# The last six output chunks of an MLP and their LayerNorm over three parts of the tokens in place of two halves, on one Trainium2 core

## The reference

```python
h = _layer_norm(ALPHA * h + (mix @ w_out + b_out), ln1_g, ln1_b)
f = jnp.square(jax.nn.relu(h @ w_mlp1 + b_mlp1)) @ w_mlp2 + b_mlp2
h = _layer_norm(ALPHA * h + f, ln2_g, ln2_b)          # y, 576 tokens x 1024

def _layer_norm(x, g, b):
    mu = jnp.mean(xf, axis=-1, keepdims=True)
    var = jnp.mean(jnp.square(xf - mu), axis=-1, keepdims=True)
    return (xf - mu) * lax.rsqrt(var + LN_EPS) * g + b
```

## Time and profile before

| | us |
|---|---|
| median of 3 runs | 827.62 |
| lowest, highest | 827.31, 828.57 |
| the profiled execution, device time | 829.96 |
| its span in the trace | 828.2 |
| its mean granted TensorE clock, share of full speed | 0.988 |

### The profile page before, as it was taken

How to read it: one execution, slowest core, us unless ns; L and a number is a source line. 1 busy time by engine, 2 the same in 40 slices (tenths; PEclk the granted TensorE clock), 3 DMA queues, 4 the chain that set the end, 5 groups by cost and what they waited for, 6 DMA issues and landing times.

```text
span 828.2 us, 14458 instructions
## 1 busy us (share of the span) xinstructions
PE 798.3 (96%) x5859; PEld 766.6 (93%) x5859; DVE 504.2 (61%) x844; ACT 390.8 (47%) x653; POOL 113.8 (14%) x134
## 2 busy tenths in 40 slices
PE   4899999999999999999999999999999999999994
PEld 2789879998988899999999999999999999999994
DVE  6753434546454456885868678774767877445454
ACT  4542425655555465563546664333554433344333
POOL 5230000190000000006550000000000000000452
PEclk9799999999999999999999999999999999999997
DMA  9503222112111202234111214222221422222202
GB/s 352 200 28 135 77 96 75 56 39 80 53 51 51 75 28 77 78 103 151 51 53 52 70 57 153 77 103 77 77 70 57 154 77 102 77 77 84 70 29 86
DMA packets 23082, 71.62 MB, mean 86 GB/s; under 512 B 2464, under 2 KB 6704, under 8 KB 22640
## 3 DMA queue, kind: packets, MB, share of 16 engines
q1 hardware_dynamic: 22192, 67.97, 24.5%
q0 software_dynamic: 544, 2.52, 0.9%
q10 hardware_dynamic: 288, 0.33, 0.1%
HBM read 65.96 MB, written 4.85 MB: 85 GB/s over the span
## 4 chain that ended last, share of the span: by engine, by line
PE 93%; DVE 5%; ACT 1%; DMA 0%; issue 0%; POOL 0%; ACTq 0%; DVEq 0%
PE lin L582 14%; PE lin L583 14%; PE lin L584 14%; PE z L1018 5%; PE z L1021 5%; PE z L1020 5%; PE lin L923 3%; PE lin L924 3%; PE lin L925 3%; PE z L797 3%; PE lin L1064 2%; PE lin L1063 2%; PE lin L1062 2%; PE z L783 1%; PE z L855 1%; PE z L584 1%
## 5 line engine op out<-in xcount | busy, mean ns | idle before, releaser
L582 PE MATMUL lin<-h_hi,whi 128*128 128x288 f32 (+1 forms) x832 | 247.2, 297 | 0.0
L583 PE MATMUL lin<-h_lo,whi 128*128 128x288 f32 (+1 forms) x832 | 245.9, 296 | 0.0
L584 PE MATMUL lin<-h_hi,wlo 128*128 128x288 f32 (+1 forms) x832 | 245.0, 294 | 0.0
L584 PEld LDWEIGHTS lin<-h_hi,wlo 128*128 128x128 f32 x832 | 156.6, 188 | 0.0
L582 PEld LDWEIGHTS lin<-h_hi,whi 128*128 128x128 f32 x832 | 156.5, 188 | 0.1
L583 PEld LDWEIGHTS lin<-h_lo,whi 128*128 128x128 f32 x832 | 156.4, 188 | 0.1
L1706 DVE TENSOR_TENSOR wlo<-raw,whi 128x1024 fp32r<-128x1024 f32 x65 | 80.9, 1245 | 34.9 <-ACT whi L1095 29.8
L1095 ACT ACTIVATE whi<-raw 128x1024 fp32r<-128x1024 f32 x58 | 60.9, 1051 | 51.1 <-PE lin L584 32.8
L1512 ACT ACTIVATE relu_t<-lin,vecs 128x288 f32<-128x288 f32 x60 | 30.0, 500 | 91.5 <-PE lin L584 88.1
L2133 DVE TENSOR_TENSOR relu_sq<-relu_t 128x288 f32<-128x288 f32 x60 | 27.5, 458 | 64.7 <-ACT relu_t L1512 64.7
L1018 PE MATMUL z<-f_ops,whi 128*128 128x288 f32 x216 | 64.2, 297 | 0.7 <-issue 0.7
(11 more groups left out here) (332 smaller groups left out, 1908.9 us busy)
## 6 DMA issues: line engine op xcount, KB each, us to landing
raw<-w_stream SPq DMA_DIRECT2D x88, 512.0 KB, 3.5
w_set<-w_sets SPq DMA_DIRECT2D x32, 384.0 KB, 3.6
r<-x_t SPq DMA_DIRECT2D x8, 296.0 KB, 5.6
y<-r SPq DMA_DIRECT2D x16, 144.0 KB, 1.9
kcache<-k_cache SPq DMA_DIRECT2D x1, 2048.0 KB, 13.9
vcache<-v_cache SPq DMA_DIRECT2D x1, 2048.0 KB, 10.5
k_new<-k_t POOLq DMA_DIRECT2D x1, 1184.0 KB, 4.8
v_new<-v_t POOLq DMA_DIRECT2D x1, 1024.0 KB, 5.7
```

Source lines behind the costliest of these rows:

```text
L582: pe.matmul(out, w_h, hi, start=first, stop=False)
L583: pe.matmul(out, w_h, lo, start=False, stop=False)
L584: return pe.matmul(out, w_l, hi, start=False, stop=last)
```

## The change

- Chunks 2 to 7 are worked on in three parts of the columns, 256, 176 and 144 wide (`PARTS2`), in place of two halves. Chunks 0 and 1 stay in halves. The products are `last_products`, the adds `add_part`, both counted by a semaphore `end_done`.
- Each part has its own sums and its own norm, interleaved on VectorE and ScalarE with the next part's adds and squares. The sums of parts 0 and 1 stand behind the first unit of the next part (`sums2`).
- In the last part GpSimd adds only up to chunk 5. Its sums, and chunk 6 with its squares, are taken up by TensorE between the products of the last unit (`last_sums`); only chunk 7 and its squares stand behind it (`last_term`, `last_square`).
- The last part's results stand in the same banks as part 0's, from column 320 on (`LATE2`). The variance is kept in PSUM (`r2_sq`) in place of SBUF (`var2`).
- The squares and sums of chunks 0 and 1 are made over the full width, once (`square2_first`, and the first two adds of GpSimd), in place of each half.
- There are 24 output DMAs in place of 16.

```diff
@@ -400,8 +402,17 @@
             return k % 6
 
         KEPT2 = 2
-        BY_DVE2 = (4, 6)
-        ADDS2 = (7, 6)
+
+        PARTS2 = (slice(0, 256), slice(256, 432), slice(432, TA))
+        LAST2 = len(PARTS2) - 1
+        BY_DVE2 = (4, 4, 6)
+
+        SUMMED2 = (KC, KC, KC - 2)
+
+        LATE2 = 320
+
+        def width2(p):
+            return PARTS2[p].stop - PARTS2[p].start
 
         def f_op(o, i, part):
 
...
+        def stat_cols(p):
+            at = LATE2 if p == LAST2 else 0
+            return slice(at, at + width2(p))
+
+        def r2_mean(p):
+            return z[:, p % 2, stat_cols(p)]
+
+        def r2_sq(p):
+            return xo[:, p % 2, stat_cols(p)]
+
+        def r2_rstd(p):
+            return small[:, stat_cols(p)] if p == 1 else z[:, 2, stat_cols(p)]
...
-            for h in range(2):
+            for p, c in enumerate(PARTS2):
                 for k in range(KC):
-                    sp.wait_ge(n2_out, KC * h + k + 1)
-                    sp.dma_start(y_out[:, k, half(h)], r2[:, k, half(h)]).then_inc(y_stored, 16)
-            sp.wait_ge(y_stored, 2 * 16 * KC)
+                    sp.wait_ge(n2_out, KC * p + k + 1)
+                    sp.dma_start(y_out[:, k, c], r2[:, k, c]).then_inc(y_stored, 16)
+            sp.wait_ge(y_stored, len(PARTS2) * 16 * KC)
...
+                    if ready is not None:
+                        pe.wait_ge(f_lo_done, ready(k))
+                    moving = f_hi[:, k, c], f_lo[:, k, c]
                     w_h, w_l = home[0][:, bass.ts(k, P)], home[1][:, bass.ts(k, P)]
-                    out = lin[:, bank, 0:HA]
                     pe.matmul(out, w_h, moving[0], start=k == 0, stop=False)
                     pe.matmul(out, w_h, moving[1], start=False, stop=False)
...
+                    last = pe.matmul(out, w_l, moving[0], start=False, stop=closes and k == KC - 1)
+                    if between is not None:
+                        between(k)
+                if not closes:
+                    pe.wait_ge(n2_first, 2)
+                    last = pe.matmul(out, ones_2[:, :], first_r2[:, c], start=False, stop=True)
+                return last
+
+            def sums2(p):
+
+                c = PARTS2[p]
+                pe.wait_ge(n2_sum[p], KC - KEPT2)
+                pe.matmul(r2_mean(p), inv_2[:, :], sum2[:, c], start=True, stop=True)
+                pe.wait_ge(n2_sumsq[p], KC - KEPT2)
+                pe.matmul(r2_sq(p), inv_2[:, :], sumsq2[:, c], start=True, stop=True).then_inc(n2_terms, 1)
+
+            def last_sums(k):
+
+                c, n = PARTS2[LAST2], SUMMED2[LAST2] - KEPT2
+                if k == 1:
+
+                    pe.wait_ge(n2_scaled, KC)
+                    pe.wait_ge(n2_sum[LAST2], n)
+                    pe.matmul(r2_mean(LAST2), inv_2[:, :], sum2[:, c], start=True, stop=False, skip_group_check=True)
+                elif k == 2:
+                    pe.wait_ge(n2_sumsq[LAST2], n)
+                    pe.matmul(r2_sq(LAST2), inv_2[:, :], sumsq2[:, c], start=True, stop=False, skip_group_check=True)
+                elif k == 3:
+                    last_term(KC - 2, False)
+                elif k == 5:
+                    last_square(KC - 2, False)
+
+            def last_term(m, stop):
+                pe.wait_ge(*r2_ready(m, LAST2))
+                pe.matmul(r2_mean(LAST2), inv_2[:, :], r2[:, m, PARTS2[LAST2]], start=False, stop=stop,
+                          skip_group_check=True)
+
+            def last_square(m, stop):
+                pe.wait_ge(n2_sq[LAST2], m - KEPT2 + 1)
+                return pe.matmul(r2_sq(LAST2), inv_2[:, :], sq2[:, m % 2, PARTS2[LAST2]], start=False, stop=stop,
+                                 skip_group_check=True)
...
+            for p, c in enumerate(PARTS2):
+                for m in range(KEPT2, KC):
+                    bank, before = out_bank(m, p)
+                    if p == 0:
+                        pe.wait_ge(lo_split, U_MLP2 + m + 1)
+                    pe.wait_ge(bank_free[bank], before)
+                    ends = p == LAST2 and m == KC - 1
+                    last_products(end_home(m), m, c, lin[:, bank, 0:width2(p)], False, None, last_sums if ends else None)\
+                        .then_inc(end_done, 1)
+                    if p and m == KEPT2:
+                        sums2(p - 1)
+            last_term(KC - 1, True)
+            last_square(KC - 1, True).then_inc(n2_terms, 1)
...
+            def square2_first(m):
+
+                if m == 0:
+                    act.wait_ge(n2_d0, 2)
+                else:
+                    for h in range(2):
+                        act.wait_ge(*r2_ready(m, h))
+                nc.scalar.activation(sq2[:, m, :], r2[:, m, :], ACT.Square).then_inc(n2_sq0, 1)
...
+            for p in range(LAST2):
+                mean2_out(p)
+                root2(p)
+                square2(2, p + 1)
+                square2(3, p + 1)
+                for k in range(KC):
+                    norm2_out(k, p)
+                    if k in (2, 5):
+                        square2(4 + k // 3, p + 1)
+                square2(6, p + 1)
+                square2(7, p + 1)
+            mean2_out(LAST2)
+            root2(LAST2)
             for k in range(KC):
-                norm2_out(k, 1)
+                norm2_out(k, LAST2)
 
...
+            def add_part(m, p):
+
+                bank, c = out_bank(m, p)[0], PARTS2[p]
+                dve.wait_ge(end_done, (KC - KEPT2) * p + m - KEPT2 + 1)
+                tt(r2[:, m, c], lin[:, bank, 0:width2(p)], r2[:, m, c], ALU.add).then_inc(bank_free[bank], 1)
...
+            def variance2(p):
+
+                dve.wait_ge(n2_msq, p + 1)
+                stt(out=r2_sq(p), in0=r2_sq(p), scalar=LN_EPS, in1=var2[:, PARTS2[p]], op0=ALU.add, op1=ALU.subtract)\
...
+                dve.wait_ge(n2_var, 2 * p + 1)
+                nc.vector.tensor_scalar(r2_sq(p), r2_sq(p), LN_EPS, None, ALU.max).then_inc(n2_var, 1)
...
+            for p in range(LAST2):
+                add_part(2, p + 1)
+                variance2(p)
+                centre2(p)
+                add_part(3, p + 1)
+                inverse2(p)
+                for k in range(KC):
+                    scale2(k, p)
+                    if k in (2, 5):
+                        add_part(4 + k // 3, p + 1)
+                add_part(6, p + 1)
+                add_part(7, p + 1)
+            variance2(LAST2)
+            centre2(LAST2)
+            inverse2(LAST2)
...
+            pool.wait_ge(n2_d0, 2)
+            for h in range(2):
+                pool.wait_ge(*r2_ready(1, h))
+            nc.gpsimd.tensor_tensor(sum2[:, :], r2[:, 0, :], r2[:, 1, :], ALU.add).then_inc(n2_sum0, 1)
+            pool.wait_ge(n2_sq0, 2)
+            nc.gpsimd.tensor_tensor(sumsq2[:, :], sq2[:, 0, :], sq2[:, 1, :], ALU.add).then_inc(n2_sumsq0, 1)
...
+            for p in range(len(PARTS2)):
+                for m in range(KEPT2, SUMMED2[p]):
+                    add2(m, p)
+                    if p and m == KEPT2:
+                        centre2(p - 1)
+            centre2(LAST2)
```

More of the change, by code:

```diff
@@ L1028, in _ @@
             mlp1(2)
[L1030 to L1055, removed]
+            def last_products(home, m, c, out, closes, ready=None, between=None):
                 for k in range(KC):
-                    if m == 0:
-                        pe.wait_ge(f_lo_done, 2 * F_TILES + 2 * k + h + 1)
-                    moving = f_hi[:, k, half(h)], f_lo[:, k, half(h)]
+                    if ready is not None:
+                        pe.wait_ge(f_lo_done, ready(k))
+                    moving = f_hi[:, k, c], f_lo[:, k, c]
@@ L1071, in _ @@
                 for h in range(2):
-                    end_half(m, h)
+                    bank, before = out_bank(m, h)
+                    if h == 0:
+                        pe.wait_ge(lo_split, U_MLP2 + m + 1)
+                    pe.wait_ge(bank_free[bank], before)
+                    ready = None if m else (lambda k, h=h: 2 * F_TILES + 2 * k + h + 1)
+                    last_products(end_home(m), m, half(h), lin[:, bank, 0:HA], m == 0, ready)\
+                        .then_inc(unit_done if h else half_done, 1)
             for h in range(2):
                 pe.matmul(r2_shift(h), ones_2[:, :], first_r2[:, half(h)], start=True, stop=True).then_inc(n2_shift, 1)
[L1075 to L1081, removed]
+            for p, c in enumerate(PARTS2):
+                for m in range(KEPT2, KC):
+                    bank, before = out_bank(m, p)
+                    if p == 0:
+                        pe.wait_ge(lo_split, U_MLP2 + m + 1)
+                    pe.wait_ge(bank_free[bank], before)
+                    ends = p == LAST2 and m == KC - 1
[5 more added lines that the diff above has]
+            last_square(KC - 1, True).then_inc(n2_terms, 1)
         @block.scalar
@@ L1637, in first_chunk2 @@
                     .then_inc(n2_first, 1)
[L1639 to L1650, removed]
@@ L2352, in variance2 @@
```

(27 more changed lines are left out.)

144 lines of the change are left out of this document (46 added, 98 removed).

## The result

| | us |
|---|---|
| before, median | 828.10 |
| after, median of 4 runs | 839.04 |
| lowest, highest after | 837.55, 839.74 |
| after / before | 1.0125, 95% interval 1.0111 to 1.0138 |
| profiled execution after, its span | 838.46, 836.7 |

The change makes the kernel 10.4 us slower by the ratio (9.2 to 11.4 by its interval); the two medians alone lie 10.9 apart. The forecast was 10.0, or 837.6 us as a time, and the median is 1.4 over that.

The account below looks back on a forecast made before the run. TensorE's stream of products, then a serial tail, was taken to bound the kernel, with weight loads pacing short products. Stream +12.9 and tail -2.9 gave +10.0 us, 837.6 us against the median 827.62; own range 834.5 to 840, extended to 841.

Parts of the forecast that it names:

- The load as the pitch: Products of parts 1 and 2: each costs a weight load, 0.111 us, so 300 take 33.3 us.
- Part 0: First part, 256 columns: 150 products of 0.1192 us each, 17.9 us.
- The sums on TensorE: Sums between products: 0.86, 0.60 and 0.98 us, paid in full, 2.44 against 0.97, +1.5 us.
- Waits: TensorE's stream waiting for other engines: chunk 5's bank 0, at most 0.5; part 1 nothing, at most 1 us.
- The stream as a whole: TensorE up to the last product's start T: products +11.4 and sums +1.5, +12.9 us.
- The tail: From the last product's start T to the end: T + 10.9 against T + 13.8, -2.9 us.
- The outputs: Last eight output DMAs: SyncE issues them 0.498 us apart whatever the columns, seven steps 3.49 us.
- Rival 1: Short products cost by columns: stream 41.6 us, +1.9, total +0.5, 828.1 us, no change; its full chance isn't legible.
- Rival 2: Products at columns plus 0.0025 us, and output issue shrinks too: 822.0 us, faster; chance 0.03.
- rival 3: Load bounds the stream and the other engines' order adds waits, 1.5 to 3 us: 840 us; chance 0.09.
- Rival 4: Granted clock falls in parts 1 and 2, products at 1.2 GHz, +10.5 us: 848 us; chance 0.03.
- The range: Forecast's own range 834.5 to 840 us, from pitch -1.2 to +1.2, tail -1.6 to +0.9, waits up to 1.

Follow-up runs that it names:

- e2_64_columns: The changed kernel, but in parts 1 and 2 the products move only the first 64 columns of the part: 864.89 us, ratio 1.0437.

## Why the prediction was right

- **The load as the pitch.** Right, and it is the main cause: of the stream's +13.4 us the products are 11.5, since 300 of them take 0.111 each, the sums 1.5 and one wait 0.4; the tail takes 3.25 off. From 790.37 to one product past T there are 35.89 us in the profile after; less 2.46 of sums this is 33.4 for them, forecast 33.3. The two runs with narrowed operands show the cause, not only the number: the pitch follows the columns once the load is halved, and it stays, as long as the clock is at 1.00, when only the moving columns are cut.
- **Part 0.** 18.15 us, of which 0.29 are a wait; 17.9 forecast for the products.
- **The sums on TensorE.** 0.87, 0.60 and 0.99 us, forecast 0.86, 0.60 and 0.98. That they are paid in full was argued in the prediction. That moving the last part's sums brings nothing was not: the prediction held that the last sum starts with the square's end because the sums queued ahead of it "move away". The kernel with the sums behind shows the same start without moving them, since at 144 columns they are short enough to end in time.
- **Waits.** The one that I had named and put at 0 (at most 0.5) came: chunk 5's unit in part 0 waits for the bank behind the weight splits, 781.40 where 781.11 was due. The others didn't come; GpSimd's last sum of part 0 ended 0.6 us before TensorE asked for it.

```profile
780.99 0.28 PE L1060 MATMUL lin<-first_r,ones 128*128 128x256 f32 x1
781.40 0.36 PE L1053 MATMUL lin<-f_hi,whi 128*128 128x256 f32 x1
```

- **The stream as a whole.** +13.4 where +12.9 was forecast: that wait, and 0.1 in the pitch. This miss and the tail's go opposite ways, so that +10.1 in the traces lies closer to the forecast's 10.0 than its terms do; that closeness is luck, the mechanism isn't.
- **The tail.** -3.25 where -2.9 was forecast, by steps that miss in both directions. The square's end was T + 0.98 (forecast 0.94), the variance T + 1.58 (1.41, though the prediction's own terms, 0.94 and 0.44, give 1.38: I left out that two sums which aren't queued ahead are slower, 0.35 us apart and not 0.245, and the last one's reader starts 0.55 after it and not 0.44), variance to centring 0.90 (0.98: the floor took 0.23 in PSUM), first scaling T + 4.45 (4.35), first output DMA T + 5.29 (5.19).
- **The outputs.** The mechanism was right, its size 0.3 off: the last DMA starts 3.2 us after the first and not 3.5, since SyncE's issues of this width are 0.47 apart and not 0.498. The end follows 2.04 after it and not 2.23. The prediction gave the rows of a transfer as the reason why the issue wouldn't shrink; the DMA of two chunks, with twice the rows, was issued in no more time, so that reason isn't borne out.
- **The rivals.** Rival 1, by columns, and the price it would have had are what the kernel with half weights shows when the load is made to hide. Rival 2 is out. The waits of rival 3 were 0.3 us and not 1.5. Rival 4 didn't happen in this kernel and did in another. Its price of +10.5 us was too low: it slowed the products and left the load as it was. At the measured 0.213 us the 300 short products would take 63.9 us, 30.6 more than forecast.
- **The range.** By the prediction's own terms (-1.2 and -1.6 down, +1.2, +0.9 and 1 up) it is 834.8 to 840.7 and not 834.5 to 840; the median of 839.04 lies in either.

Work that stands behind the last product, but ends while other engines are on their serial chain, costs nothing there, and costs its full length when it is moved into a stream without gaps. In a serial tail, look also at what issues the outputs: a queue that needs half a microsecond per DMA hides the gain of narrower work, and fewer, larger DMAs gave 0.9 us of it back at 144 columns, where ScalarE was well ahead of the queue, and next to nothing at 288.

## What the runs showed of the hardware

- The pitch of a product goes by columns alone when the load hides: 0.0667 us at 144, 0.0817 at 176, 0.1325 at 288, 0.1833 at 400, that is 0.458 to 0.464 ns a column. I had taken it as 1/2.4 ns a column and 0.0125 us on top, which is right at 288 only.
- The granted clock can fall to 0.50 while TensorE is never idle in the profile: in `e2_64_columns` the products of 64 columns with full loads begin at 790.04, the clock fell between 797 and 798, and the loads then took 0.213 us. It held at 1.00 through 36 us with 176 and 144 columns. What makes the difference is open.
- SyncE issued output DMAs of one chunk 0.47 us apart at 144 columns and 0.50 at 288; one of two chunks took no longer to issue (0.37 us), but its end came 0.2 us later at 144 columns and 0.3 at 288.
